# Splitting the first weight block's transfer and moving its low half to GpSimd in a one-core, three-layer kernel

## The reference

```
h = x                                             # 256 x 1024, float32
u = rms_norm(h, conv_norm_g)
a = u @ w_pw1 + b_pw1                             # 1024 x 2048: the first weights that are used
u = a[..., :1024] * sigmoid(a[..., 1024:])
u = depthwise_conv(u, dw_w, 31 taps) + dw_b
h = h + silu(layer_norm(u)) @ w_pw2 + b_pw2
...                                               # feed-forward, ple: gate * (p[i] @ ple_w_proj[i])
q, k, v = split(rms_norm(h, attn_norm_g) @ w_qkv)
probs = softmax(q k^T + bias, causal), two of them for each head
w = probs[:, :, 0] - lam * probs[:, :, 1]
o = w @ v                                         # for each head, 256 x 128
h = h + rms_norm(o, sub_g) * (1 - lambda_init) @ w_o
...
```

## Time and profile before

| | before |
|---|---|
| three runs | 1038.81, 1035.30, 1035.13 us, median 1035.3 us |
| profiled execution | 1035.07 us |
| its span | 1033.3 us, so 1.8 us lie around it |
| busy share of the span | PE 99%, PEld 84%, DVE 62%, ACT 50%, POOL 11% |
| granted TensorE clock, mean | 0.999 of full |
| transfers | 191.67 MB, mean 186 GB/s |

### The profile page before, as it was taken

One profiled execution on the slowest core, in us unless ns is written; L12 is line 12 of the kernel. 1 busy time (PEld: TensorE's weight loads), 2 busy tenths in 40 slices (PEclk: granted clock), 3 DMA queues, 4 the chain that ended last, 5 costly groups with the idle time before them and its releaser, 6 DMA issues.

```text
span 1033.3 us, 13513 instructions
## 1 busy us (share of the span) xinstructions
PE 1022.6 (99%) x5510; PEld 864.1 (84%) x5510; DVE 638.0 (62%) x802; ACT 517.7 (50%) x635; POOL 109.5 (11%) x88
## 2 busy tenths in 40 slices
PE   8999999999999999999999999999999999999997
PEld 8977888888888888888888888788888888999886
DVE  5996654545557667765555456676454557777564
ACT  5437544343466668653444446754544453344433
POOL 4991100000020320010000002100000000000000
PEclk9999999999999999999999999999999999999999
DMA  8865865554543632565555544655555445554531
GB/s 322 247 220 102 276 229 169 197 203 167 200 163 139 228 122 82 204 242 187 196 172 201 190 177 163 228 207 197 193 189 183 158 164 204 180 187 166 204 120 41
DMA packets 30669, 191.67 MB, mean 186 GB/s; under 512 B 3720, under 2 KB 6280, under 8 KB 8720
## 3 DMA queue, kind: packets, MB, share of 16 engines
q1 hardware_dynamic: 25056, 179.06, 48.3%
q0 software_dynamic: 2096, 7.79, 3.3%
q10 hardware_dynamic: 3456, 3.97, 1.4%
HBM read 187.58 MB, written 3.21 MB: 185 GB/s over the span
## 4 chain that ended last, share of the span: by engine, by line
PE 97%; DMA 1%; ACT 1%; DVE 1%; issue 0%; POOL 0%; SPq 0%; POOLq 0%; ACTq 0%
PE bank L282 30%; PE bank L284 30%; PE bank L283 30%; PE bank L324 2%; PE bank L499 1%; PE bank L399 1%; DMA raw<-in_ws 1%; PE bank L593 0%; PE bank L690 0%; PE bank L727 0%; PE bank L614 0%; PE bank L509 0%; ACT arena L1209 0%; PE bank L594 0%; ACT w_hi L936 0%
## 5 line engine op out<-in xcount | busy, mean ns | idle before, releaser
L1424 DVE TENSOR_TENSOR w_lo<-raw,w_hi 128x2048 fp32r<-128x2048 f32 x157 | 359.3, 2291 | 209.8 <-ACT w_hi L936 208.2
L936 ACT ACTIVATE w_hi<-raw 128x2048 fp32r<-128x2048 f32 x168 | 320.9, 1910 | 161.6 <-PE bank L284 151.6
L282 PE MATMUL bank<-w_hi,x_hi 128*128 128x512 f32 x800 | 317.6, 397 | 0.2
L284 PE MATMUL bank<-w_hi,x_lo 128*128 128x512 f32 x800 | 312.4, 391 | 0.0
L283 PE MATMUL bank<-w_lo,x_hi 128*128 128x512 f32 x800 | 311.5, 389 | 0.0
L282 PEld LDWEIGHTS bank<-w_hi,x_hi 128*128 128x128 f32 x800 | 150.2, 188 | 34.3 <-issue 3.9
L284 PEld LDWEIGHTS bank<-w_hi,x_lo 128*128 128x128 f32 x800 | 150.2, 188 | 32.2
L283 PEld LDWEIGHTS bank<-w_lo,x_hi 128*128 128x128 f32 x800 | 150.4, 188 | 29.2
L282 PE MATMUL bank<-w_hi,z_hi 128*128 128x512 f32 (+1 forms) x368 | 143.5, 390 | 0.1
L284 PE MATMUL bank<-w_hi,z_lo 128*128 128x512 f32 (+1 forms) x368 | 141.8, 385 | 0.0
L283 PE MATMUL bank<-w_lo,z_hi 128*128 128x512 f32 (+1 forms) x368 | 141.6, 385 | 0.0
(11 more groups left out here) (227 smaller groups left out, 757.4 us busy)
## 6 DMA issues: line engine op xcount, KB each, us to landing
raw<-in_ws SPq DMA_DIRECT2D x169, 1024.0 KB, 4.8
arena<-u_scr ACTq DMA_DIRECT2D x16, 142.0 KB, 5.6
arena<-in_rows POOLq DMA_DIRECT2D x2, 1024.0 KB, 4.7
toep<-bias_row POOLq DMA_DIRECT2D x1, 1536.0 KB, 35.4
h<-in_x_tok SPq DMA_DIRECT2D x2, 512.0 KB, 4.9
arena<-in_rows POOLq DMA_DIRECT2D x2, 512.0 KB, 5.4
arena<-toep POOLq DMA_DIRECT2D x1, 1024.0 KB, 9.2
arena<-in_pool_m POOLq DMA_DIRECT2D x1, 768.0 KB, 4.5
```

What stands on the lines that cost most here:

```text
L282: pe.matmul(dst, s_hi, m_hi, start=first, stop=False)
L284: return pe.matmul(dst, s_lo, m_hi, start=False, stop=last)
L936: act.activation(w_hi[:, g % SPLIT, :], raw[:, g % RAW, :], ACT.Copy).then_inc(hi_done, 1)
L1424: dve.tensor_tensor(w_lo[:, g % SPLIT, :], raw[:, g % RAW, :], w_hi[:, g % SPLIT, :].bitcast(F32), ALU.subtract).then_inc(lo_done, 1)
```

## The change

Six edits. (1) SP starts `prm` behind the two token tiles; before, ACT started it. (2) Piece 0 comes in two transfers of 128 x 1024, the first with the semaphore `raw_first`. (3) Both low halves of piece 0 are made by POOL, one after the other; DVE makes none. (4) `lam_t` is started by POOL behind them, and ACT starts the two ple inputs (`p_t0`, `p_t1`) behind the `w_hi` of piece 2; the `w_hi` of piece 1 now stands behind the `x_hi` of the blocks (1, t). (5) `keep_busy` at the beginning has 19 matmuls, not 23. (6) At the attention's end, the steps are written in another order, and `values` waits for each head's weights apart.

```diff
             for t in range(TT):
                 sp.dma_start(h[:, t, :], x_tok[t * P:(t + 1) * P, :]).then_inc(S(f"ld_h{t}"), 16)
-            for g in range(NPIECE):
+            sp.dma_start(prm[:, :], par).then_inc(S("ld_par"), 16)
+            sp.dma_start(raw[:, 0, 0:D], ws[0][:, 0:D]).then_inc(S("raw_first"), 16)
+            sp.dma_start(raw[:, 0, D:HALF], ws[0][:, D:HALF]).then_inc(raw_loaded[0], 16)
+            for g in range(1, NPIECE):
...
-            keep_busy(23, 7)
+            keep_busy(19, 7)
...
                     pe.wait_ge(S("v_copied"), 2 * (pair // 2) + 2)
-                    pe.wait_ge(S("w_copied"), 2 * pair + 2)
                     for i in range(2):
                         hd = 2 * pair + i
+                        pe.wait_ge(S("w_copied"), hd + 1)
...
-            for step in (values(0), weights(5), weights(6), values(1), weights(7), values(2), values(3)):
+            for step in (values(0), weights(5), values(1), weights(6), values(2), weights(7), values(3)):
...
             pool.dma_start(onehot_t[:, :], onehot).then_inc(S("ld_bias"), 16)
-            pool.dma_start(lam_t[:, :, :], bass.AP(lam_rows.tensor, 0, [[0, P], [HD, 4], [1, HD]])).then_inc(S("ld_lam"), 16)
...
-            pool.wait_ge(S("first_lo_a"), 1)
+            pool.wait_ge(S("first_hi"), 1)
+            pool.tensor_tensor(w_lo[:, 0, 0:D], raw[:, 0, 0:D], w_hi[:, 0, 0:D].bitcast(F32), ALU.subtract) \
+                .then_inc(S("first_lo_a"), 1)
             pool.wait_ge(hi_done, 1)
             pool.tensor_tensor(w_lo[:, 0, D:HALF], raw[:, 0, D:HALF], w_hi[:, 0, D:HALF].bitcast(F32), ALU.subtract) \
                 .then_inc(S("first_lo_b"), 1)
+            pool.dma_start(lam_t[:, :, :], bass.AP(lam_rows.tensor, 0, [[0, P], [HD, 4], [1, HD]])).then_inc(S("ld_lam"), 16)
...
-            act.dma_start(prm[:, :], par).then_inc(S("ld_par"), 16)
...
-            act.dma_start(p_t0, p_feat[0]).then_inc(S("ld_p0"), 16)
-            act.dma_start(p_t1[:, :, :], p_feat[1]).then_inc(S("ld_p1"), 16)
-            act.wait_ge(raw_loaded[0], 16)
...
-            dve.wait_ge(S("first_hi"), 1)
-            dve.tensor_tensor(w_lo[:, 0, 0:D], raw[:, 0, 0:D], w_hi[:, 0, 0:D].bitcast(F32), ALU.subtract) \
-                .then_inc(S("first_lo_a"), 1)
```

More of the change, by code:

```diff
@@ L1069, in _ @@
             act.activation(x_s[:, 0, :], h[:, 0, :], ACT.Copy, scale=st2[:, 48:49]).then_inc(S("x_scaled"), 1)
+            act.wait_ge(S("raw_first"), 16)
+            act.activation(w_hi[:, 0, 0:D], raw[:, 0, 0:D], ACT.Copy).then_inc(S("first_hi"), 1)
+            h_split("x", 0)
+            act.wait_ge(raw_loaded[0], 16)
+            act.activation(w_hi[:, 0, D:HALF], raw[:, 0, D:HALF], ACT.Copy).then_inc(hi_done, 1)
+            fed[0] = 1
+            h_split("x", 1)
+            feed(2)
             act.dma_start(p_t0, p_feat[0]).then_inc(S("ld_p0"), 16)
             act.dma_start(p_t1[:, :, :], p_feat[1]).then_inc(S("ld_p1"), 16)
-            act.wait_ge(raw_loaded[0], 16)
[L1073 to L1079, removed]
             def sigmoid(f):
```

## The result

The changed kernel takes 1038.61 us (median of 20 executions, 1036.44 to 1040.38) against 1035.27 us before (20 executions on the same chip). The ratio is 1.0024, 95% interval 1.0017 to 1.0032. So it is 3.3 us slower, where 0.6 us faster was forecast; the time lies outside both ranges that the prediction gives, and nearest to rival 4 (1039.5). The profiled execution took 1038.17 us, with a span of 1036.3 us.

A forecast was written before the change was run, and what follows sets the result against it. PE, busy 99% of the span, was taken to bound the kernel. The start's -0.5 and the attention's -0.1 us gave 1034.5 profiled, 1034.7 as median; own range 1034.0 to 1035.2, over rivals 1 to 3 1033.6 to 1037.0.

The forecast's parts named there:

- rival 4: Start: PE loses its clock level in the gap that rival 1 opens; +3 us, 1039.5 us; chance 0.04.
- Part 1: Start: `prm` behind the tokens lets ACT scale 0.6 us earlier, at 8.3; bounds 0 and 0.7 us.
- part 3: Start: 19 instead of 23 `keep_busy` let PE's transposes go at 9.5 instead of 10.1 us.
- Part 2: Start: piece 0 in two transfers, first half landed at 7.1 us, so its `w_hi` runs 9.4 to 10.4.
- Part 4: Start: low halves on POOL; DVE's second `x_lo` precedes POOL's second half; n = 0 at 14.2, n = 1 at 17.6, gain 0.5 us.
- rival 1: Start: POOL's second half goes before DVE's second `x_lo`; n = 1 1.2 us later, 1036.5 us; chance 0.27.
- Part 5: After the start: moved ple inputs and `lam_t` cost nothing; piece 1's low part stays hidden by 0.4 us.
- Part 6: Attention's end: PE's 0.7 us wait goes, but the next work is bound too; gain 0.1 us, bounds 0 and 0.7.

The follow-up runs named there:

- e6: The kernel before with one edit: SP starts `prm` behind the tokens, ACT no longer does; 1034.83 us, ratio 0.9995.
- e3: The changed kernel with one more wait: POOL starts its second low half only when both `x_lo` of blocks (0, t) are there; 1035.44 us.
- e4: The kernel before with both low halves of piece 0 on POOL and nothing else; 1040.46 us, ratio 1.0046.
- e13: The changed kernel with the ple inputs and `lam_t` started at their old, early places; 1038.03 us, ratio 1.0023.
- e1: The changed kernel with the first low half of piece 0 on DVE again, POOL making only the second; 1037.84 us, ratio 1.0016.
- e7: e1 with the ple inputs and `lam_t` started at their old, early places; 1034.09 us, ratio 0.9985 to the kernel before.
- e5: The kernel before with the attention edit alone; 1035.22 us, ratio 0.9997.
- e8: e1 with only `lam_t` back at its old, early place, the ple inputs still late; 1035.16 us, ratio 1.0003 to the kernel before.
- e11: e7 with `sigmoid(1)` moved ahead of `spread(4)` and `p_split(0)`; 1035.42 us, ratio 0.9998 to the kernel before.
- e2: The changed kernel with 18 instead of 5 `keep_busy` matmuls ahead of piece 0; 1038.19 us, ratio 1.0028 to the kernel before.
- e12: e2 with the ple inputs and `lam_t` back at their old, early places; 1038.05 us, ratio 1.0024 to the kernel before.
- e14: e7 with SP holding weight pieces 6 and 12 back until the first and last `u_scr` stores land; 1042.90 us, ratio 1.0068 to the kernel before.
- e15: e1 with SP holding weight pieces 6 and 12 back until the first and last `u_scr` stores land; 1043.19 us, ratio 1.0071 to the kernel before.
- e16: e12 with SP holding weight pieces 6 and 12 back until the first and last `u_scr` stores land; 1045.62 us, ratio 1.0093 to the kernel before.

## Why the prediction was wrong

1. **Part 1** had the direction right and the size too small: 0.91 us for the scaling (7.99 against 8.90), above my bound of 0.7. Taken alone (e6), `prm` moved the rest of the start by only 0.18 us and the median by 0.4 (an interval that reaches over no change), since the later `keep_busy` and the whole piece hold it, as part 3 said.
2. **Part 2** failed in its estimate that the first half piece has landed at 7.1. It was issued at 2.11 and took 7.8 us, so the first `w_hi` half began at 9.89 and not at 9.4. The sum counted 1.89 MB until then; 2.60 MB had moved by 9.8, as SP had started the second half and pieces 1 to 3 from 2.59 on, and they share the 16 engines.
3. **Part 3** held: the transposes started at 9.20 behind ACT's scaling (9.5 forecast), with a wait of 0.2 us.
4. **Part 4** is the step that failed. The exclusion itself was read rightly: the pair of `x_lo` waited for POOL, as in the earlier trace rows. The choice "in this step I take DVE" was wrong. POOL's request at 12.94 (11.90 + 1.04) stood before POOL's first half was over, and its second half began in the handover at 13.45. With DVE first (e3) n = 0 starts nearly as forecast (14.35, against 14.2); rival 1 had the mechanism and the place right. But e3 doesn't bring the forecast gain either: POOL's second half ran from 14.40 to 16.81 and not from 14.0 to 16.3, n = 1 started at 18.06 and not at 17.6, and the time is 1035.4. Some of that is e3's own wait, so how much of the 0.5 us was there to be had isn't shown. The Trainium skill ("SBUF — State Buffer", section "Who interferes with whom": whoever issues first holds the ports for the whole instruction) pointed to POOL here. The changed kernel's trace agrees: POOL's row begins at 13.45, that of the second `x_lo` at 13.96. So do e3 and e4. I weighed it at 0.27 because DVE's two rows usually follow without a gap; the pairs of 5.28 us here and 5.27 in e4 show that POOL's instruction can stand between them.
5. **Rival 4** had the clock's fall right, its price too high (3 us; measured 1.5, as the lower level lasted 3.4 us and not six) and a chance of 0.04 that was far too small. Its total came within 0.9 us of the median partly by luck. It needed only rival 1, and a still PE for 2.9 us. Rival 1's 1.2 us, the 1.5 of the clock and the 0.5 by which part 2 was late make 3.2, against the 3.3 that the start cost.
6. **Part 5** said "nothing" for the moved transfers, and named PE waits between 20 us and the attention as what would prove it wrong. In the changed kernel's own profile there is none for a transfer (its waits of 0.5 and 0.2 us on DVE near 87 stand in the kernel before too), and e13 puts their price at 0.6 us or less. In e1, where the start was as fast as hoped, they raised the stalls (1037.84 against 1034.09 in e7). I had followed their readers and not what shares the DMA engines with them. The margin of piece 1 was never tried, as n = 1 came late.
7. **Part 6** held: e5's last matmul stands at 1026.84 as before, although its start was 0.08 us later: 0.1 us gained, as forecast, with the short wait in front of `o_jobs` that was forecast too. In the changed kernel 0.3 was saved, within the bounds of 0 and 0.7.

Why a piece issued at 24.3 us takes 4.8 us in one kernel and 7.7 in another stays partly open. In e1 the piece before it took 8.1 us, in e8 6.3; but e11's started as early as e8's, had its transfers early, and took 7.3. e7 and e11 are the same program up to 27 us, so some of it changes from one execution to the next. That is a likely source of the single executions at 1037 to 1039 us in many of the kernels here, the one before too, but it was not isolated. Beside the experiments, 23 of 105 executions of the kernel before took over 1037 us; 20 of these have a mean granted clock of 0.995 to 0.997, where the faster ones have 0.998 to 1.000.

## What to carry to other kernels

Before giving GpSimd a subtraction from SBUF, look for a DVE subtraction with both inputs in SBUF that is due in the same microseconds, and assume that the waiting GpSimd instruction goes in between two of DVE's; one wait on DVE's result, as in e3, decides the order. A gap of 2.9 us in front of TensorE was paid twice here, once as idle time and once at the lower clock level. A small store whose landing an engine waits for was at least as late here as the large transfer in front of it, so an edit that gains a microsecond at the start can lose it 50 us later, where the two no longer miss each other; e7, which gains at the start and leaves the transfers early, has the lowest median here, 1034.09 us.

## What the runs showed of the hardware

- A GpSimd instruction that waited went between two queued DVE instructions that exclude it: the pair of 128 x 512 `x_lo` took 5.28 and 5.27 us instead of 1.29, while GpSimd's 128 x 1024 took 2.78 instead of 2.36. GpSimd's row began at 13.45, that of the DVE instruction that came behind it at 13.96.
- After 2.9 us of standing still PE ran at 0.50 of full clock from about 17.5 to 20.8 us; in e2 and e12, where `keep_busy` filled the same time, it read 1.00 throughout. PE's waits of 1.2 and 1.5 us near 74 us in e1 went with a mean of 0.83 over 10 us, and 64 matmuls took 5.35 us instead of 3.66.
- A 144 KB store on ACT's queue took 5.3 us with a 1 MB piece of SP's queue in flight that had 4.9 us to go (e1). With nothing in flight it took 1.8 us in e14 and e15, and 3.2 in e16.
- The second of two 1 MB pieces issued 0.5 us apart after a hold took 10.6 us (e14), beside four spreads of 142 KB; the pieces of the kernel before near 25 and 63 us took 4.7.
